# The down projection of a feed-forward layer by seven block products for eight

## What is computed

```python
FFN_DIM = 2816
h = rms_norm_2(x, norm_ffn_pre[l])
u = causal_dwconv(h @ ffn_w_up[l], ffn_conv_w[l]) + ffn_conv_b[l]
gate, up = jnp.split(u, 2, axis=-1)
x = x + rms_norm_2((jax.nn.silu(gate) * up) @ ffn_w_down[l], norm_ffn_post[l])
```

## Time and profile before

| | |
|---|---|
| three runs, us | 2386.51, 2387.25, 2390.12 |
| median, us | 2387.25 |
| the profiled execution, us | 2386.57 |
| its span, us | 2384.8 |
| its mean granted TensorE clock | 0.993 |

### The profile page before, as it was taken

How to read it: one execution, slowest core, us unless ns; L and a number is a source line. 1 busy time by engine, 2 the same in 40 slices (tenths; PEclk the granted TensorE clock), 3 DMA queues, 4 the chain that set the end, 5 groups by cost and what they waited for, 6 DMA issues and landing times. The chain is left out here.

```text
span 2384.8 us, 33134 instructions
## 1 busy us (share of the span) xinstructions
PE 2317.7 (97%) x12824; PEld 1890.1 (79%) x12824; DVE 1259.8 (53%) x1772; ACT 1063.5 (45%) x2262; POOL 601.8 (25%) x415
## 2 busy tenths in 40 slices
PE   7999999899999999999999999999999999999999
PEld 4887787778887787778888887677888888888887
DVE  5955205875544502795550466550787777774121
ACT  5444333773535323684434454553653333334221
POOL 2200110332310021132421130112214444465130
PEclk9999999999999999999999999999999999999999
DMA  7432110113212120103211100003222222237231
GB/s 255 150 125 71 36 53 1 37 49 128 71 47 88 36 71 18 36 1 124 89 53 30 58 1 10 19 10 140 98 81 80 80 80 88 90 133 250 86 132 45
DMA packets 139073, 181.87 MB, mean 76 GB/s; under 512 B 8700, under 2 KB 102307, under 8 KB 138917
## 3 DMA queue, kind: packets, MB, share of 16 engines
q1 hardware_dynamic: 137877, 179.74, 22.2%
q10 hardware_dynamic: 1040, 0.00, 0.0%
HBM read 151.41 MB, written 28.31 MB: 75 GB/s over the span
## 5 line engine op out<-in xcount | busy, mean ns | idle before, releaser
L856 PE MATMUL ps<-w_hi,hT_hi 128*128 128x512 f32 (+1 forms) x384 | 142.2, 370 | 2.1 <-PEq L4649 1.0
L856 PE MATMUL ps<-w_lo,hT_hi 128*128 128x512 f32 (+1 forms) x384 | 142.1, 370 | 0.0
L856 PE MATMUL ps<-w_hi,hT_lo 128*128 128x512 f32 (+1 forms) x384 | 142.1, 370 | 0.0
L856 PE MATMUL ps<-hT_hi,w_hi 128*128 128x512 f32 x360 | 140.5, 390 | 0.0
L4139 POOL TENSOR_TENSOR w_lo<-ffn_sums,w_hi 128x512 fp32r<-128x512 f32 x76 | 96.8, 1298 | 171.8 <-ACT w_hi L4321 171.8
L856 PE MATMUL ps<-hT_lo,w_hi 128*128 128x512 f32 x360 | 140.1, 389 | 0.0
L787 POOL TENSOR_TENSOR w_lo<-difp_raw,w_hi 128x2048 fp32r<-128x2048 f32 x8 | 36.8, 4604 | 386.0 <-ACT w_hi L756 386.0
L856 PE MATMUL ps<-hT_hi,w_lo 128*128 128x512 f32 x328 | 127.7, 389 | 0.0
L4189 PE MATMUL ps<-ffn_t_hi,w_hi 128*128 128x512 f32 x304 | 118.4, 389 | 0.7 <-DVE ffn_u L4498 0.7
L4189 PE MATMUL ps<-ffn_t_hi,w_lo 128*128 128x512 f32 x304 | 118.3, 389 | 0.0
L4189 PE MATMUL ps<-ffn_t_lo,w_hi 128*128 128x512 f32 x304 | 118.3, 389 | 0.0
(11 more groups left out here) (576 smaller groups left out, 6483.6 us busy)
## 6 DMA issues: line engine op xcount, KB each, us to landing
ffn_raw<-in_ffn_w_up SPq DMA_DIRECT2D x40, 512.0 KB, 4.6
mix_gla<-in_w_ada SPq DMA_DIRECT2D x32, 512.0 KB, 3.5
ffn_raw<-in_ffn_w_down SPq DMA_DIRECT2D x30, 512.0 KB, 4.7
xres<-big SPq DMA_DIRECT2D x24, 512.0 KB, 2.6
hid<-ffn_f SPq DMA_DIRECT2D x22, 512.0 KB, 2.6
ffn_sums<-hid SPq DMA_DIRECT2D x44, 256.0 KB, 3.8
glap_raw<-in_w_in SPq DMA_DIRECT2D x10, 1024.0 KB, 5.4
difp_raw<-in_w_in SPq DMA_DIRECT2D x10, 1024.0 KB, 5.0
```

The lines of the kernel that those rows point to most:

```text
L856: mm = nc.tensor.matmul(out, l, r, start=(job.part != 1 and c == 0 and k == 0), stop=(job.evac and c == job.chunks - 1 and k == len(pairs) ...
```

## The change

The down product becomes a 2x2 block product too: halves of the tokens, of the 22 feature chunks (11 steps each) and of the output columns. Seven products r = 0 to 6 of 11 steps each (`DOWN`) take the place of eight; a step is now one left operand (128 x 512 tokens) and one right operand (128 x 512 columns), 12 matmuls into four banks. Left operands are the features or one of four sums of feature blocks, right operands the weights or one of four sums of weight blocks.

- Feature sums: DVE makes them in the up phase (`feature_sums(q)`, four operations of 128x512 on SBUF), in stage 0 and in the odd stages 1 to 17 and once behind the last feature; SP stores them to `hsum`, 1 MB each, 11 times. The feature chunks are made in another order (`feature_chunk`), so that the chunks k and k + 11 follow each other, and `f` has two buffers.
- Weight sums: in eleven stages SP loads 1 MB of down weights (`load_parts`), POOL makes the sums (`part_sums(k)`, four operations of 128x512), in its queue behind low part 7(k+2)+2, and SP stores them to `wsum` (1 MB).
- In the down phase each step loads 256 KB left and 256 KB right, with five staging buffers each, ACT makes two high parts, POOL the left low part and for the first six steps the right one too, DVE the other right ones; 16 steps of operands are held.
- Results of finished products are copied or added into SBUF by ACT (`product_out`) and DVE (`combine`); the norm works on them. For the last product DVE adds PSUM to the partial result before the square.

The core of the diff:

```diff
+DOWN = (("a11", "b11", 0, True), ("s2", "t2", 1, True), ("a12", "b21", 0, False), ("s3", "t3", 1, False),
+        ("s1", "t1", 0, True), ("a22", "t4", 1, False), ("s4", "b22", 0, False))
+NK = NF // 2
+NDOWN = NPROD * NK
...
+    STAGED, POOLED, RING, AHEAD, LAST = 5, 6, 16, 12, 6
```

SP, in the up phase:

```diff
             for j in range(PLAIN, NF - 1):
+                if j % 2:
+                    store_feature_sums((j - 3) // 2)
                 store(j - 1)
+                if j - PLAIN - 1 in range(NK):
+                    store_parts(j - PLAIN - 1)
                 if j + 3 < NF:
                     load(j + 3)
+                if j - PLAIN < NK:
+                    load_parts(j - PLAIN)
```

POOL:

```diff
+            def part_sums(k):
+                b11, b12, b21, b22 = (down.parts(i) for i in range(4))
+                pool.wait_ge(s_wload, 32 * (k + 1))
+                pool.tensor_tensor(b11, b12, b11, ALU.subtract).then_inc(s_wsum, 1)
...
             for n in range(ALLPROD):
                 low(n)
+                s, k = divmod(n, NPROD)
+                if k == 2 and s - 2 in range(NK):
+                    part_sums(s - 2)
```

PE, a step of the down phase:

```diff
+            def step(n, i):
+                r, k = divmod(n, NK)
+                (a_hi, a_lo), (b_hi, b_lo) = down.unit(n, 0), down.unit(n, 1)
                 toks = slice(P * i, P * i + P)
+                for j, (l, r_) in enumerate(((a_hi, b_hi), (a_hi, b_lo), (a_lo, b_hi))):
+                    mm = nc.tensor.matmul(ps[:, down.BANKS[DOWN[r][2]][i], :], l[:, toks], r_,
```

DVE, in the up phase and, last, behind the last product:

```diff
+            def feature_sums(q):
+                a11, a21, a12, a22 = (f[:, c, h] for c in range(2) for h in halves)
+                s1, s2, s3, s4 = (down.feature_sums(q)[:, k, :] for k in range(4))
+                dve.wait_ge(s_f, 2 * q + 2)
+                if q:
+                    dve.wait_ge(s_fst, 16 * q)
+                nc.vector.tensor_tensor(s1, a21, a22, ALU.add).then_inc(s_fsum, 1)
+                nc.vector.tensor_tensor(s3, a11, a21, ALU.subtract).then_inc(s_fsum, 1)
+                dve.wait_ge(s_fsum, 4 * q + 1)
+                nc.vector.tensor_tensor(s2, s1, a11, ALU.subtract).then_inc(s_fsum, 1)
+                dve.wait_ge(s_fsum, 4 * q + 3)
+                nc.vector.tensor_tensor(s4, a12, s2, ALU.subtract).then_inc(s_fsum, 1)
...
                 add(u_half(0, 1), u_half(1, 0), s, 1, s_q2)
+                if s == 0:
+                    feature_sums(0)
                 feature(j - 1)
...
                 add(u_half(1, 1), u_half(1, 1), s, 2, s_c22)
+                if s % 2:
+                    feature_sums((s + 1) // 2)
                 dve.wait_ge(s_prod, NPROD * s + 6)
                 add(u_half(1, 0), u_half(1, 0), s, 1, s_c21)
...
+            for i in range(4):
+                dve.wait_ge(s_fin, i + 1)
+                nc.vector.tensor_tensor(y12[:, i, :], y12[:, i, :], ps[:, down.BANKS[0][i], :], ALU.add).then_inc(s_y12, 1)
```

More of the change, by code:

```diff
@@ L3947, in staged_h @@
[L3947 to L3960, removed]
+    SUMS = ("s1", "s2", "s3", "s4")
@@ new lines, in of, with unit, freed_by, staged @@
+    def of(self, name, c):
+        return [t[:, c, :] for t in self.up.tokens(name)]
+    def unit(self, m, right):
+        return self.units[2 * (m % self.RING) + right][0]
+    def freed_by(self, m, right):
+        return self.units[2 * m + right][1]
+    def staged(self, m, right):
+        k = m % self.STAGED
+        if right:
+            return self.up.raw[:, k // 4, 512 * (k % 4):512 * (k % 4) + 512]
+        return self.up.sums[:, (k // 4 + NWINO) % 2, k % 4, :]
+    def row(self, up, half):
+        return self.hid[P * up:P * up + P, 512 * half:512 * half + 512]
@@ new lines, in source @@
+    def source(self, m, right):
+        r, k = divmod(m, NK)
+        name = DOWN[r][right]
+        if name in self.SUMS:
+            c = 512 * self.SUMS.index(name)
+            return self.hsum[P * k:P * k + P, c:c + 512]
+        if name in self.PARTS:
+            c = 512 * self.PARTS.index(name)
+            return self.wsum[P * k:P * k + P, c:c + 512]
+        one, two = int(name[1]) - 1, int(name[2]) - 1
+        if right:
+            k, half = k + NK * one, two
+            return self.w_down[P * k:P * k + P, 512 * half:512 * half + 512]
+        return self.row(k + NK * two, one)
@@ L4113, in _ @@
                     sp.wait_ge(s_st, 16 * NF)
+                    sp.wait_ge(s_fst, 16 * NK)
                     load_row(2)
[L4115 to L4126, removed]
@@ new lines, in product_out, with square, first_share @@
+            def product_out(r, dst, signal):
+                act.wait_ge(s_step, NK * (r + 1))
+                for i in range(4):
+                    nc.scalar.activation(dst[:, i, :], ps[:, down.BANKS[0][i], :], ACT.Copy).then_inc(signal, 1)
+            def square(x, half, src, done):
+                i = tiles[x]
+                act.wait_ge(s_sq, done)
+                nc.scalar.activation(junk, src, ACT.Square, accum_out=ssq[:, half, i:i + 1]).then_inc(s_sq, 1)
+            def first_share(x, half, done):
+                i = tiles[x]
+                act.wait_ge(s_sq, done)
+                own.mark(nc.scalar.activation(bias[:, i:i + 1], ssq[:, half, i:i + 1], ACT.Identity,
+                                              bias=m.eps[:, 0:1], scale=1.0 / D))
@@ new lines, in right_low, with combine @@
+            def right_low(n):
+                dve.wait_ge(s_bhi, n + 1)
+                hi, lo = down.unit(n, 1)
+                nc.vector.tensor_tensor(lo, down.staged(n, 1), hi.bitcast(F32), ALU.subtract).then_inc(s_blov, 1)
+            def combine(r, dst, left, signal):
+                dve.wait_ge(s_step, NK * (r + 1))
+                for i in range(4):
+                    nc.vector.tensor_tensor(dst[:, i, :], left[:, i, :], ps[:, down.BANKS[DOWN[r][2]][i], :],
+                                            ALU.add).then_inc(signal, 1)
```

483 lines of the change are left out of this document (276 added, 207 removed).

## The result

The changed kernel takes 2416.5 us (median of 4 executions, 2411.5 to 2418.5), the kernel before 2386.9 in the same session: ratio 1.0118, interval 1.0099 to 1.0136. It is 29.6 us slower. Forecast were 2395 and at most 2406. The sign was right, the size was not.

The account below looks back on a forecast made before the run. PE was taken to bound the kernel, busy 2317.7 of 2384.8 us. Fewer matmuls -29.9, waits +37.2 and tail +0.7 summed to +8.0 us, giving 2395 us, range 2374 to 2406.

Parts of the forecast that it names:

- Down products: Down phase: 924 matmuls for 1056, 132 fewer at an unchanged 0.2267 us each, -29.9 us.
- Weight sums: Up phase: POOL's sums run across DVE's gate convolution, 0.95 us lost in each of five odd stages, +4.7 us.
- feature sums: Up phase: DVE's sums take turns with POOL; 4.8 us lost per even stage 2 to 12, first 4.0, +28.0 us.
- The last three stages: End of up phase: feature sums of stages 13, 15, 17 meet POOL's low parts, +3.5 us in all.
- rivals on the port: Up phase: uninterrupted DVE sums keep the port, 2374 us, chance 0.13; or waits cost 1.3 us each, 2410 us, 0.08.
- The Trainium skill's rule named in the prediction: SBUF: DVE instructions with two SBUF inputs and GpSimd instructions reading SBUF exclude each other; loser blocked for the whole instruction.
- 0.91: Last up stage, earlier trace: microseconds a DVE gate convolution operation was taken to wait for POOL's present one, not 1.30.
- Traffic: Up phase: added loads and stores through DRAM fit a 19.04 us stage, SP's queue is covered; counted at nothing.
- Down phase: Down phase: operand work on POOL, ACT, DVE and loads keep ahead of PE; nothing lost, bounds 0 and 2 us.
- Tail: End of kernel: the last tile takes its PSUM add ahead of the square, +0.7 us.

Follow-up runs that it names:

- both short: Changed kernel with feature sums of pairs 1 to 9 and all POOL weight sums cut to one column, all transfers kept: 2363.4 us, 0.9900 of before.
- waits filled: Changed kernel with 20 useless matmuls ahead of the fourth product's wait in stages 2, 4, 6, 8, 10, 12: 2403.2 us, 1.0071 of before.
- weight sums placed: Changed kernel with POOL's weight sums two low parts earlier, behind a wait for DVE's gate convolution, their load earlier on SP: 2404.1 us, 1.0069 of before.
- all three together: Changed kernel with feature sums spread over two stages, weight sums behind the gate convolution, first three output rows stored before further residual loads: 2387.6 us, 1.0000 of before.
- weight sums short: Changed kernel with POOL's weight sums cut to one column instead of 512, transfers kept: 2376.4 us, 0.9958 of before.

## Why the prediction was right and wrong

Its total was +8.0, measured are +29.6. By its steps, from the two profiled executions:

1. *Down products*, -29.9: right (239.1 to 209.2).
2. *Weight sums* and 3. *feature sums*, waits of 37.2 us, with stage 0 and the last stages in it: right in mechanism but for the last stage, and the size near. Waits rose by 42.5 - 0.8 = 41.7. Even stages have 4.84 to 4.87 for the 4.8 forecast, the first 4.32 for 4.0, stage 0 1.02 for 1.0; the odd ones 0.96 to 1.77 for 0.95. The higher value is three meetings for two: the first gate operation was assumed to slip through, as at 2122.71 in the earlier trace rows, but there POOL's operation had just 0.23 us to go, and here, with 0.6 to 1.3 to go, it takes 1.13 to 1.82 (read from the rows, not tried by itself). The last three stages were put at 3.5 and cost 1.45 + 1.44 + 3.38 - 0.84 = 5.4: the first two are near the 1.3 forecast, the last met no turn in its gate convolution and lost 2.06 to ACT's copy instead. By its own terms the prediction's last stage would have been 2.2 + 3 x 0.91 - 0.86 - 0.95 = 3.1, and the three 5.7, so its 3.5 doesn't follow from them. Its rivals on the port are out as priced: the sums don't keep it (1.4 to 1.8 us each), and a wait costs what is left of POOL's operation, 0.73 and 1.07 in both short, and not always 1.30. The Trainium skill's rule named in the prediction is borne out by this: DVE was blocked to the end of POOL's operation, within 0.02 us. The prediction was wrong to read 0.91 against it; a whole 1.30 would take an operation of DVE that is issued together with POOL's.
4. *Traffic*, nothing: right for the transfers themselves (both short: at most 0.4 us). POOL has no wait for a load of down weights. Not right for SP's queue: in the last stage the loads of down operands stand behind the store of late sums, and that is the way by which the 2.06 us reach DVE.
5. *Down phase*, nothing: right.
6. *Tail*, +0.7: the mechanism named is there, the size is +4.2. The add was seen; that SP serves rows as store, landing, load, landing, now with transfers of 5 us and no down phase over most of them, was not.

**The step that failed** is the sum under 2 and 3. It charged PE for the wait and nothing for what follows: it took 0.2267 us for every matmul behind it, with the clock of 1.00 that the earlier trace rows show for ten stages without a wait. A wait of nearly 5 us cost 1.7 to 2.8 us more in slow matmuls, the seven long waits (3.4 to 4.9 us) 14.8 together, the short ones 0.13 each: 15.9 in all, 15.8 more than before (waits filled gives back 11.6 of it). With that term and the tail as measured the sum would have been -29.9 + 41.7 + 15.8 + 4.2 = +31.8, against 29.6 measured by medians. So of the miss of 21.6 us the clock is 15.8, the tail's row order 3.5, and the waits 4.5, 2.1 of them by ACT's copy in the last stage. The profiled pair shows 25.0, because the changed kernel's profiled execution happened to reach its first Winograd product 6.8 us earlier; nothing before that product is changed, and the other profiled kernels show it from 1774.3 to 1780.0 us.

What stays open: why the clock falls behind one wait and not behind the next of the same length (waits of 2.1 to 2.2 us; with the weight sums placed it fell behind two of six waits of 2.9; all three together, not behind the one of 3.36), and the 2 us between 31.8 and 29.6.

## What to carry to other kernels

Price an idle PE by the wait and by the matmuls behind it: here waits of 1 us cost themselves, waits of nearly 5 half as much again, and two or three short waits are cheaper than one long one. Before work is moved to "free" engines, write down which of them meet on SBUF operands, instruction by instruction; shares of busy time (DVE 59, POOL 30 per cent) say nothing about it, and the price of a turn is what is left of the other's operation. Look as well at who waits in a queue behind a late result: a store of sums held up loads, these a copy, and this the add. Shrinking an operation to one column, with its transfers left in place, tells within one run whether arithmetic or traffic is to blame.

## What the runs showed of the hardware

- A DVE operation of one column with two SBUF inputs took 1.22 us beside POOL and 0.15 alone, and ended 0.02 us behind POOL's; without pauses between them two such streams alternate strictly, and POOL's operations get longer too (1.29 to 1.62 to 1.74, and 2.24 beside the gate convolution at 1911.27).
- A TENSOR_SCALAR from SBUF to SBUF takes 0.75 us on 1024 columns when POOL stands still or its operation has 0.2 us left, and up to 1.82 when it has more: 0.55 us over what is left. Means hide this: with the weight sums short its 18 cases have a mean of 1.288 and lie between 0.75 and 1.81. Where POOL's operations follow each other at the opening of the down phase, it waits for several: 3.35 us in the changed kernel beside three of them, 5.67 with both short beside five.
- The granted clock stayed at the 2.4 GHz level behind waits up to 1.9 us, fell behind some of 2.1 to 2.9, and behind all seven of 3.4 to 4.9 in the changed kernel; behind one of 3.36 (all three together) it stayed.
